# Recurrence levels of a gated linear recurrence: matmuls over the later half of each block, one copy a level, a third level buffer, and the key decays ahead of the query decays

## The chip, the cores and the metric

The kernel runs on one core of one Trainium2 chip. The metric is the device time of one execution in microseconds, the median of a few runs. The two hybrid layers of one inference step are computed in that one launch, for a prompt of 512 tokens (with 16 learned tokens ahead of it, 528 in all) and for 8 sample tokens (536 columns in all).

## The reference, cut to what matters

Each layer has a sparse attention branch and a gated linear recurrence branch (4 heads, key size 128, value size 128). The change lies in the recurrence, where a score between a query position t and an earlier key position s has its own decay for each of the 128 key dimensions:

```python
def gla_chunk(S0, q, k, v, logf):
    b = jnp.cumsum(logf.astype(jnp.float32), axis=1)
    causal = jnp.tril(jnp.ones((C, C), dtype=bool))
    diff = b[:, :, None] - b[:, None, :]
    decay = jnp.exp(jnp.where(causal[None, :, :, None, None], diff, -jnp.inf))
    scores = jnp.einsum('bthk,bshk,btshk->bths', q, k, decay)
    o = jnp.einsum('bths,bshv->bthv', scores, v) + jnp.einsum('bthk,bhkv->bthv', q * jnp.exp(b), S0)
    b_last = b[:, -1]
    S = jnp.exp(b_last)[..., None] * S0 + jnp.einsum('bshk,bshv->bhkv', k * jnp.exp(b_last[:, None] - b), v)
    return o, S
```

## The kernel before, in words

Five instruction streams (PE, DVE, ACT, POOL, SP) run a hand-written order with semaphores. A layer is: input projections (weights are split into a high and a low part, so each product is three matmuls, L695), index scores and top-k, attention, then the recurrence, the two branch projections, the output projection and the feed-forward part. The recurrence needs the whole of PE's, DVE's and ACT's attention; no projection is laid beside its level stage.

The recurrence works on chunks of 128 positions (four, and a tail of 16). `B[:, 0:4]` holds the queries, `B[:, 4:8]` the running sums of the log decays, `B[:, 8:12]` the values, `K` the keys, all with the key dimension on the partitions. The decayed scores inside a chunk are built in **levels**: `HALVES` = 64, 32, 16, 8, 4, 2, 1 are half-block sizes for levels 0 to 6, and level 7 is the diagonal, without a decay. For each level:

- DVE takes the differences of the log decays to the middle of each block: `xv[later half] = b - mid` (L2022), `xv[earlier half] = mid - b` (L2023), into the buffer `X[lev % 2]` (`X0` or `X1`);
- ACT takes the exponential of the whole buffer (L1387);
- DVE multiplies the later halves by the queries (L2034) and the earlier halves by the keys (L2035);
- PE multiplies, for each of 4 heads and 4 chunks, the 128 columns of the buffer by the same 128 columns (L1014): 16 matmuls of 128x128 by 128 columns in f32, as two groups of 8 (`hp` 0 and 1), each of which fills one PSUM work buffer of 1024 columns; a small matmul group for the tail of 16 follows at levels 3 to 7 (L1020);
- DVE copies what counts of each work buffer into `Asc` under the 8-bit mask of the level (`level_scores`, L2001, 1024 columns a copy), and the tail into `Atail` (L2008).

In the profile an f32 matmul of L1014 has two records, so a level shows as 32.

There are two work buffers of PSUM. `items` lists all their uses in order; an item takes buffer number (place % 2), and PE begins an item (`begin`) only when the item two places before it has been drained. Between the levels PE turns the values of one chunk (`v_turn`, transposes through L658), which ACT drains into `v_tok`.

DVE's order in the loop over the levels (L2011 and on) is: differences of the level, copy of the first half of the level before, then, after ACT's exponential, the two products, and the copy of the second half of the level before. At level 0 the places of the copies are taken by the low parts of the attention output (L2029) and by the diagonal.

After the last level ACT takes the exponential of the running sums into `X1` (L1401), DVE multiplies the queries by it (L2040, `q_decayed`), ACT writes 20 exponentials for the keys into the same `X1` (L1405, `k_exp`), and DVE multiplies them by the keys (L2044, `k_decayed`). PE then turns the decayed keys of chunk 0 (L658), computes the outputs of the chunk (`rec_out`, L1067 and L1068) and its state update (L1073), and one head of the sample tokens (`rank1` L1043, `rec_sample` L1051). SP loads the sample states `s0` (L501) when `k_decayed` is there, since they lie over `K`, and stores them (L388).

Each projection's gates went to DRAM; SP brings both halves back into `normed` with two DMAs (L473) early in the attention. They are first used at L2079 (half 0) and L2113 (half 1), after the recurrence.

Of the kernel before, what the change touches and what calls it, by code (L numbers as in the profile page):

```python
# [76 lines left out]
def build(nc, t, out):  # L77
# [83 lines left out]
    with ctx:  # L161
# [8 lines left out]
        normed = sb("normed", [P, 2, KT, T], f32r)  # L170
# [48 lines left out]
        base = (nc.sbuf_base + 63) // 64 * 64  # L219
        size = nc.sbuf_usable_end - base  # L220

# [50 lines left out]
        X = [X0, X1]  # L272
# [125 lines left out]
        def _(sync):  # L398
# [34 lines left out]
            with sync.Fori(0, DEPTH) as L:  # L433
# [33 lines left out]
                for n in range(4):  # L467
                    load_merge(n)
                for e in range(2):
# [20 lines left out]
                for h in range(4):  # L490
# [5 lines left out]
                    else:  # L496
# [156 lines left out]
        def _(pe):  # L653
# [16 lines left out]
            with pe.Fori(0, DEPTH) as L:  # L670
# [332 lines left out]
                for place_no, lev in enumerate(LEVELS):  # L1003
                    if lev < 7:
                        wait(pe, "lev_ready", L, 14, 2 * lev + 2)
                        left = right = X[lev % 2]
# [3 lines left out]
                    for hp in range(2):  # L1010
                        ps = begin(("level", lev, hp))
                        for m in range(8):
                            h, c = 2 * hp + m // 4, m % 4
                            mm = pe.matmul(ps[:, m * P:(m + 1) * P], left[:, h, c * P:(c + 1) * P],  # L1014
                                           right[:, h, c * P:(c + 1) * P], start=True, stop=True)
                        finish(mm, ("level", lev, hp))
# [7 lines left out]
                    if place_no < 5:  # L1024
                        r0, n = TILES[place_no]
                        ps = begin(("v_turn", place_no))
                        for h in range(4):
                            mm = transpose(ps[0:n, h * P:(h + 1) * P], B[:, 8 + h, r0:r0 + n])
                        finish(mm, ("v_turn", place_no))
                    elif place_no < 7:  # L1030
                        name, src = (("v_sample", B[:, 8:12, TP:T]), ("k_sample", K[:, :, TP:T]))[place_no - 5]
                        ps = begin(name)
                        for h in range(4):
                            mm = transpose(ps[0:NB, h * P:(h + 1) * P], src[:, h, :])
                        finish(mm, name)
# [114 lines left out]
        def _(act):  # L1150
# [26 lines left out]
            with act.Fori(0, DEPTH) as L:  # L1177
# [197 lines left out]
                for n in range(4):  # L1375
# [7 lines left out]
                    act.activation(att_hl[:, 0, n, :], A[:, n, :], ACT.Copy).then_inc(S["att_hi"], 1)  # L1383
                for lev, hs in enumerate(HALVES):
# [3 lines left out]
                    if lev < 5:  # L1388
                        n = TILES[lev][1]
                        drain_to(v_tok[0:n, lev, :], ("v_turn", lev), src=work[slot_of(("v_turn", lev))][0:n, 0:512])  # L1390
                    elif lev == 5:
                        drain_to(v_s[:, :], "v_sample", src=work[slot_of("v_sample")][0:NB, 0:512])
                    else:
# [3 lines left out]
                wait_filled(act, L, ("level_tail", 5))  # L1397
# [3 lines left out]
                act.activation(X1[:, :, :], B[:, 4:8, 0:TP], ACT.Exp).then_inc(S["decay_last"], 1)  # L1401
# [807 lines left out]
```

## Time and profile before

| | us |
|---|---|
| median of 3 runs | 2376.68 |
| lowest and highest | 2375.5, 2708.09 |
| the profiled execution, its own time | 2378.47 |
| its span, first to last instruction | 2376.5 |
| mean granted TensorE clock | 0.928 of full |

The level stage of layer 0 lies at 560.7 to 635.5 us of the span, that of layer 1 at 1721.0 to 1796.2 us. Durations are those of the one profiled execution. A row of a timeline that ends in "xN" merges N instructions: its first number is the start of the first, its second the time in which they were busy, and what is in brackets is the idle time of the engine ahead of it. "PE" are matmuls, "PEld" their weight loads, which can run under the matmuls ahead.

### The profile page before, as it was taken

What the parts mean: (1) busy time and instruction counts of PE and PEld (TensorE: products, weight loads), DVE (VectorE), ACT (ScalarE), POOL (GpSimd) and SP (SyncE); (2) the same over time, 40 slices, a digit from 0 to 9 for tenths busy, and PEclk for the clock granted to TensorE, in tenths of its full rate; (3) what the DMA queues carried; (4) which work ended last, traced back from release to release, by engine and by line L of the source; (5) the groups of instructions that cost most, each with busy time, mean ns of one, the idle gap of its engine ahead of it and who ended that gap; (6) DMA issues with size and microseconds to landing.
All of it is one profiled execution on the core that took longest, in us unless ns stands there. A gap on an engine that the chain in (4) does not pass through costs nothing.

```text
span 2376.5 us, 43282 instructions
## 1 busy us (share of the span) xinstructions
PE 2138.7 (90%) x15670; PEld 1995.6 (84%) x15670; DVE 1263.9 (53%) x2379; ACT 775.1 (33%) x1187; POOL 762.1 (32%) x414
## 2 busy tenths in 40 slices
PE   3999899886698999999999898997758989999998
PEld 2987799755588999999999778995557989999998
DVE  3475577658645643045337566875684654421433
ACT  3233222254323433222333232224522334322224
POOL 1632247200014443444355222650000344434433
PEclk9998999777879999999999799998787999999999
DMA  4322135300023322232241212432002223223322
GB/s 121 101 81 54 45 98 176 105 33 1 28 78 95 89 88 75 85 97 78 72 144 56 72 45 72 147 115 105 1 1 74 88 82 89 86 66 104 88 62 80
DMA packets 308948, 188.87 MB, mean 79 GB/s; under 512 B 15680, under 2 KB 295328, under 8 KB 307776
## 3 DMA queue, kind: packets, MB, share of 16 engines
q1 hardware_dynamic: 299168, 160.03, 23.6%
q0 software_dynamic: 4224, 16.78, 2.0%
q10 hardware_dynamic: 5408, 10.16, 1.3%
q8 instruction: 84, 1.38, 0.2%
q14 instruction: 64, 0.52, 0.1%
HBM read 167.47 MB, written 18.10 MB: 78 GB/s over the span
## 4 chain that ended last, share of the span: by engine, by line
PE 64%; issue 17%; DVE 9%; POOL 5%; ACT 3%; SPq 1%; DVEq 1%; DMA 1%; POOLq 0%; ACTq 0%
PE acc L695 49%; POOL w_lo L555 4%; PE work L658 3%; PE work L982 3%; PE work L1014 1%; PE acc L959 1%; PE work L924 1%; DVE Asc L2001 1%; POOL k_sel L621 1%; DVE std L1606 1%; ACT E L1355 1%; PE work L721 1%; PE work L1051 1%; DVE merged L2106 1%; PE work L1067 1%
## 5 line engine op out<-in xcount | busy, mean ns | idle before, releaser
L555 POOL TENSOR_TENSOR w_lo<-raw,w_hi 128x1024 fp32r<-128x1024 f32 (+3 forms) x290 | 631.1, 2177 | 1515.6 <-ACT w_hi L1193 1514.6
L695 PE MATMUL acc<-normed,w_hi 128*128 128x268 f32 x5696 | 967.1, 292 | 26.4 <-POOL w_lo L555 22.8
L695 PEld LDWEIGHTS acc<-normed,w_hi 128*128 128x128 f32 x5696 | 810.6, 192 | 58.2 <-issue 43.9
L1193 ACT ACTIVATE w_hi<-raw 128x1024 fp32r<-128x1024 f32 (+1 forms) x290 | 293.1, 1011 | 966.8 <-PE acc L695 959.4
L695 PE MATMUL acc<-normed,w_lo 128*128 128x268 f32 x2848 | 589.8, 289 | 0.0
L695 PEld LDWEIGHTS acc<-normed,w_lo 128*128 128x128 f32 x2848 | 450.9, 191 | 0.0
L695 PE MATMUL acc<-hidden,w_hi 128*128 128x268 f32 x1408 | 236.0, 290 | 16.1 <-DVE hidden L2152 16.1
L695 PEld LDWEIGHTS acc<-hidden,w_hi 128*128 128x128 f32 x1408 | 201.2, 192 | 16.9 <-issue 16.9
L695 PE MATMUL acc<-hidden,w_lo 128*128 128x268 f32 x704 | 146.4, 290 | 0.0
L2152 DVE TENSOR_TENSOR hidden<-act_f,hidden 128x536 f32 x44 | 89.5, 2033 | 54.0 <-ACT hidden L1466 54.0
L2145 DVE TENSOR_TENSOR silu<-silu,rnorm 128x536 f32<-128x536 f32 x44 | 83.4, 1896 | 59.1 <-ACT silu L1463 59.1
L695 PEld LDWEIGHTS acc<-hidden,w_lo 128*128 128x128 f32 x704 | 111.9, 192 | 0.0
L695 PE MATMUL acc<-merged,w_hi 128*128 128x268 f32 x512 | 87.1, 293 | 14.0 <-DVE merged L2106 14.0
L2127 DVE TENSOR_TENSOR x<-acc,x 128x536 f32<-128x536 f32 x32 | 22.9, 717 | 131.1 <-PE acc L695 131.1
L695 PEld LDWEIGHTS acc<-merged,w_hi 128*128 128x128 f32 x512 | 74.3, 195 | 14.4 <-issue 14.4
L2162 DVE TENSOR_TENSOR x<-acc,x 128x536 f32 x16 | 11.5, 716 | 137.6 <-PE acc L695 137.6
L1014 PE MATMUL work<-X 128*128 128x128 f32 x448 | 67.0, 321 | 17.5 <-DVE Asc L2001 17.5
L1014 PEld LDWEIGHTS work<-X 128*128 128x128 f32 x448 | 65.7, 237 | 19.1 <-DVE Asc L2001 11.3
L658 PEld LDWEIGHTS work<-cst,E 128*128 128x128 f32 (+2 forms) x240 | 26.0, 153 | 61.4 <-issue 60.9
L2142 DVE TENSOR_TENSOR silu<-acc,rnorm 128x536 f32<-128x536 f32 x44 | 31.5, 717 | 84.9 <-PE acc L695 84.1
L2148 DVE TENSOR_TENSOR act_f<-acc,silu 128x536 f32<-128x536 f32 x44 | 31.5, 716 | 80.3 <-PE acc L695 80.0
L1183 ACT ACTIVATE relu<-work 128x256 f32<-128x256 f32 (+3 forms) x64 | 33.1, 517 | 124.6 <-PE work L839 124.6
(320 smaller groups left out, 3031.9 us busy)
## 6 DMA issues: line engine op xcount, KB each, us to landing
raw<-in_w_in_dram SPq DMA_DIRECT2D x90, 512.0 KB
raw<-in_w_gu_dram SPq DMA_DIRECT2D x88, 512.0 KB
raw<-in_w_down_dram SPq DMA_DIRECT2D x32, 384.0 KB
raw<-in_w_down_dram SPq DMA_DIRECT2D x32, 320.0 KB
gate_scratch<-gate_out ACTq DMA_DIRECT2D x32, 268.0 KB
normed<-gate_scratch SPq DMA_DIRECT2D x4, 2144.0 KB, 10.7
raw<-in_w_o_dram SPq DMA_DIRECT2D x16, 512.0 KB
raw<-in_w_pa_dram SPq DMA_DIRECT2D x16, 256.0 KB
```

Source lines behind the costliest of these rows:

```text
L555: pool.tensor_tensor(w_lo[s][:, 0:kt, :], raw[slot][:, 0:kt, :], w_hi[s][:, 0:kt, :].bitcast(f32), ALU.subtract).then_inc(lo_done, 1)
L621: pool.indirect_dma_start(dst[:, i, :], None, rows, bass.IndirectOffsetOnAxis(row_idx[:, i:i + 1].bitcast(u32), 0))\
L658: return pe.transpose(dst, src, ident[0:k, 0:k])
L695: mm = pe.matmul(acc[o][:, half, 0:HT], w[s][:, k, :], mov[:, part, k0 + k, half * HT:(half + 1) * HT], start=start and n == 0, stop=stop ...
L982: mm = pe.matmul(ps[64 * s:64 * s + 64, 0:n], tok[0:w, c, 256 + n2 * 64:320 + n2 * 64], pT[0:w, s, c, 0:n], start=c == 0, stop=c == j)
L1014: mm = pe.matmul(ps[:, m * P:(m + 1) * P], left[:, h, c * P:(c + 1) * P], right[:, h, c * P:(c + 1) * P], start=True, stop=True)
L1183: act.activation(dst, ps if src is None else src, func, **kw).then_inc(drained[slot_of(item)], 1)
L1193: act.activation(w_hi[slot % 2][:, 0:kt, :], raw[slot][:, 0:kt, :], ACT.Copy).then_inc(hi_done, 1)
L2142: TT(halves(silu[:, :]), acc[0][:, :, 0:HT], halves(rnorm[:, :]), ALU.mult).then_inc(taken[0], 1)
L2145: TT(silu[:, :], silu[:, :], rnorm[:, :], ALU.mult).then_inc(S["up_scaled"], 1)
L2148: TT(halves(act_f[:, :]), acc[1][:, :, 0:HT], halves(silu[:, :]), ALU.mult).then_inc(taken[1], 1)
L2152: TT(hidden[:, 1, ds(g, 1), :].rearrange("p a t -> p (a t)"), act_f[:, :], hidden[:, 0, ds(g, 1), :].rearrange("p a t -> p (a t)").bitcast ...
```

## The change

PE's matmuls at levels 0 to 6 move only the columns of the later halves (64 of 128 for each head and chunk, taken with a stride), so a level fills one work buffer instead of two. DVE copies them with one `copy_predicated` of 1024 columns a level instead of two; its mask and its destination are taken with the same stride. The level buffers rotate over three (`X2` lies in the second half of `normed`), the differences of the next level are taken ahead of the products of this one, and the copy of a level comes after the products of the next. The gates' second half comes back only after `q_decayed`, since `X2` lies where it goes. Three `v_turn` come behind the diagonal, the other turns behind levels 0 to 3. After the levels ACT makes the key decays first, and DVE multiplies the keys before the last copy and the queries after it; the query decays go through `X2`.

```diff
-    turns = [("v_turn", c) for c in range(5)] + ["v_sample", "k_sample"]
+    TURNS = {0: [("v_turn", 0), ("v_turn", 1), ("v_turn", 2)], 1: [("v_turn", 3)], 2: [("v_turn", 4)], 3: ["v_sample"],
+             4: ["k_sample"]}
     for n, lev in enumerate(LEVELS):
-        items += [("level", lev, 0), ("level", lev, 1)] + ([("level_tail", lev)] if lev >= 3 else []) + turns[n:n + 1]
+        items += [("level", 7, 0), ("level", 7, 1)] if lev == 7 else [("level", lev)]
+        items += ([("level_tail", lev)] if lev >= 3 else []) + TURNS.get(n, [])
...
+        X2 = nc.alloc_sbuf_tensor_at("X2", [P, 4, TP], f32, offset=base_n + KT * TB)
+        X = [X0, X1, X2]
...
-                for e in range(2):
-                    sync.dma_start(normed[:, e, :, :].bitcast(f32), gate_dram[:, :, e, :].rearrange("g p t -> p g t"))\
-                        .then_inc(S[f"gate_back{e}"], 16)
+                gate_return(0)
...
+                    if h == 1:
+                        wait(sync, "q_decayed", L, 1, 1)
+                        hold(sync)
+                        gate_return(1)
                     if h >= 1:
                         store_state(sync, L, h - 1)
...
+                        left = right = X[lev % 3]
+                        ps, hs = begin(("level", lev)), HALVES[lev]
+                        for m in range(16):
+                            h, c = m // 4, m % 4
+                            late = right[:, h, c * P:(c + 1) * P].rearrange("p (b t) -> p b t", t=2 * hs)[:, :, hs:]
+                            mm = pe.matmul(ps[:, m * 64:(m + 1) * 64].rearrange("p (b t) -> p b t", t=hs),
+                                           left[:, h, c * P:(c + 1) * P], late, start=True, stop=True)
+                        finish(mm, ("level", lev))
...
                 for lev, hs in enumerate(HALVES):
                     w = 512 if hs >= 16 else TP
                     wait(act, "lev_diff", L, 14, 2 * lev + 2)
-                    act.activation(X[lev % 2][:, :, 0:w], X[lev % 2][:, :, 0:w], ACT.Exp).then_inc(S["lev_exp"], 1)
+                    act.activation(X[lev % 3][:, :, 0:w], X[lev % 3][:, :, 0:w], ACT.Exp).then_inc(S["lev_exp"], 1)
+                    if lev == 0:
+                        for c in range(3):
+                            v_drain(c)
...
-                wait_filled(act, L, ("level_tail", 5))
+                wait_filled(act, L, ("level_tail", 4))
...
-                act.activation(X1[:, :, :], B[:, 4:8, 0:TP], ACT.Exp).then_inc(S["decay_last"], 1)
-                wait(act, "q_decayed", L, 1, 1)
                 for c, (r0, n) in enumerate(TILES):
                     for h in range(4):
                         act.activation(X1[:, h, r0:r0 + n], B[:, 4 + h, r0:r0 + n], ACT.Exp, scale=-1.0,
                                        bias=B[:, 4 + h, r0 + n - 1:r0 + n]).then_inc(S["k_exp"], 1)
+                wait_filled(act, L, ("level_tail", 5))
+                act.activation(X2[:, :, :], B[:, 4:8, 0:TP], ACT.Exp).then_inc(S["decay_last"], 1)
...
+                def level_scores(lev):
+
+                    hs = HALVES[lev]
+                    ps = wait_filled(vec, L, ("level", lev))
+                    hold(vec)
+                    late = level_mask[:, lev, :].rearrange("p (b t) -> p b t", t=2 * hs)[:, :, hs:]
+                    drain_ins(vec.copy_predicated(
+                        Asc[:, :, :].rearrange("p h (c b t) -> p (h c) b t", c=4, t=2 * hs)[:, :, :, hs:],
+                        late.unsqueeze(1).broadcast_to((P, 16, 64 // hs, hs)),
+                        ps[:, :].rearrange("p (m b t) -> p m b t", m=16, t=hs)), ("level", lev))
+                    if lev >= 3:
+                        tail_scores(lev)
...
+                level_diff(0)
+                for n in range(4):
+                    wait(vec, "att_hi", L, 4, n + 1)
+                    TT(att_hl[:, 1, n, :], A[:, n, :], att_hl[:, 0, n, :].bitcast(f32), ALU.subtract)\
+                        .then_inc(S["att_lo"], 1)
+                wait(vec, "att_lo", L, 4, 4)
+                hold(vec)
+                level_diff(1)
+                wait(vec, "scores_cleared", L, 2, 2)
+                diagonal(0)
+                diagonal(1)
+                tail_scores(7)
+                level_product(0)
+                for lev in range(1, 7):
+                    if lev < 6:
+                        level_diff(lev + 1)
+                    level_product(lev)
+                    level_scores(lev - 1)
                 wait(vec, "lev_ready", L, 14, 14)
-                wait(vec, "decay_last", L, 1, 1)
-                TT(B[:, 0:4, 0:TP], X1[:, :, :], B[:, 0:4, 0:TP], ALU.mult).then_inc(S["q_decayed"], 1)
-                level_scores(6, 0)
-                level_scores(6, 1)
                 wait(vec, "k_exp", L, 20, 20)
                 TT(X1[:, :, :], X1[:, :, :], K[:, :, 0:TP], ALU.mult).then_inc(S["k_decayed"], 1)
+                level_scores(6)
+                wait(vec, "decay_last", L, 1, 1)
+                TT(B[:, 0:4, 0:TP], X2[:, :, :], B[:, 0:4, 0:TP], ALU.mult).then_inc(S["q_decayed"], 1)
```

`level_diff` and `level_product` hold the same two instructions each as before (L2022, L2023 and L2034, L2035), and `diagonal` the copy of level 7.

## Rows read from the trace of the kernel before

**Rows 1.** The page's busy shares, and one of its costliest groups (parts 1 and 5).

```profile
PE 2138.7 (90%) x15670; PEld 1995.6 (84%) x15670; DVE 1263.9 (53%) x2379; ACT 775.1 (33%) x1187; POOL 762.1 (32%) x414
...
L2001 DVE COPY_PREDICATED Asc<-level_mask,work 128x1024 f32<-128x1024 uint8 x32 | 41.2, 1295 | 12.1 <-PE work L1014 12.1
```

**Rows 2.** Windows of both stages: length, busy PE, PEld, DVE, ACT, POOL, clock, DMA, GB/s.

```profile
560.70:635.50 74.80, 40.67 (x301) 38.37 (x300) 60.63 (x56) 25.38 (x37) 0.00 (x0) 0.80 0.00 1
1721.00:1796.20 75.20, 39.38 (x296) 37.29 (x297) 60.84 (x57) 25.38 (x37) 0.00 (x0) 0.82 0.00 1
```

**Rows 3.** Timeline around the matmuls of level 1, layer 0.

```profile
579.54 3.84 PE L1014 MATMUL work<-X 128*128 128x128 f32 x32 [2.72 <-DVE Asc L2001]
...
581.74 1.33 DVE L2001 COPY_PREDICATED Asc<-level_mask,work 128x1024 f32<-128x1024 uint8 x1
581.76 1.91 ACT L1387 ACTIVATE X<-X 128x2048 f32<-128x2048 f32 x1 [4.31 <-DVE X L2023]
...
583.71 1.23 DVE L2034 TENSOR_TENSOR X<-X,proj_rec 128x1024 f32<-128x1024 f32 x1 [0.64 <-ACT X L1387]
...
585.99 1.28 DVE L2001 COPY_PREDICATED Asc<-level_mask,work 128x1024 f32<-128x1024 uint8 x1
```

**Rows 4.** Windows of L924's matmuls (4 moved columns) alone: length, busy, clock, DMA.

```profile
433.70:437.50 3.80, 3.80 (x36) 1.00 0.19 74
438.00:443.20 5.20, 5.20 (x26) 0.50 0.17 50
```

**Rows 5.** Timeline of L1051 (1 moved column), clock 1.00 and 0.50.

```profile
649.17 1.95 PE L1051 MATMUL work<-proj_rec,s 128*128 128x1 f32 x16
...
678.18 3.57 PE L1051 MATMUL work<-proj_rec,s 128*128 128x1 f32 x16
```

**Rows 6.** Windows of L1014's matmuls alone, with the same columns.

```profile
571.00:574.20 3.20, 3.01 (x15) 0.50 0.00 0
579.60:583.10 3.50, 3.50 (x31) 1.00 0.00 0
588.10:591.20 3.10, 3.10 (x17) 0.50 0.02 5
612.70:617.50 4.80, 4.60 (x32) 0.74 0.02 3
```

**Rows 7.** Timeline of the stage's start.

```profile
560.73 1.22 DVE L2022 TENSOR_TENSOR X<-proj_rec 128x1024 f32<-128x1024 f32 x1
...
563.00 2.59 DVE L2029 TENSOR_TENSOR att_hl<-proj_att,att_hl 128x536 fp32r<-128x536 f32 x4
...
570.29 1.11 PE L658 MATMUL work<-cst,proj_rec 128*128 128x128 f32 x4 [3.05 <-DVE Asc L2001]
...
571.44 0.60 ACT L1183 ACTIVATE v_tok<-work 128x512 f32<-128x512 f32 x1 [6.41 <-PE work L658]
```

**Rows 8.** Timeline of the stage's end.

```profile
621.39 5.37 PE L1014 MATMUL work<-X 128*128 128x128 f32 x32
...
626.75 5.57 ACT L1405 ACTIVATE X<-proj_rec 128x128 f32<-128x128 f32 x20 [2.50 <-DVE proj_rec L2040]
...
632.35 2.36 DVE L2044 TENSOR_TENSOR X<-X,K 128x2112 f32<-128x2112 f32 x1 [3.15 <-ACT X L1405]
...
635.53 0.55 PEld L1067 LDWEIGHTS work<-Asc,v_tok 128*128 128x128 f32 x2
```

**Rows 9.** Three lines: duration min/median/max in ns, first and last start, forms.

```profile
L1014 PE MATMUL work<-X x448: 273/275/426, 571.2 to 1787.1; 128*128 128x128 f32 x150
...
L1051 PE MATMUL work<-proj_rec,s x128: 250/250/373, 649.2 to 1842.0; 128*128 128x1 f32 x128
...
L2022 DVE TENSOR_TENSOR X<-proj_rec x14: 1205/1240/1247, 560.7 to 1773.5; 128x1056 f32<-128x1056 f32 x8, 128x1024 f32<-128x1024 f32 x6
```

**Rows 10.** DMA issues: size of each, median time from issue to landing.

```profile
normed<-gate_scratch SPq DMA_DIRECT2D x4, 2144.0 KB, 10.7
...
out_dram<-s SPq DMA_DIRECT2D x8, 512.0 KB, 4.0
```

More of the change, by code:

```diff
@@ L468, in _, with gate_return @@
                     load_merge(n)
+                def gate_return(e):
+                    sync.dma_start(normed[:, e, :, :].bitcast(f32), gate_dram[:, :, e, :].rearrange("g p t -> p g t"))\
+                        .then_inc(S[f"gate_back{e}"], 16)
                 for e in range(2):
@@ L1005, in _ @@
                         wait(pe, "lev_ready", L, 14, 2 * lev + 2)
-                        left = right = X[lev % 2]
+                        hold(pe)
+                        left = right = X[lev % 3]
[6 more added lines that the diff above has]
+                        finish(mm, ("level", lev))
                     else:
@@ L1009, in _ @@
                         left, right = K, B
[L1010 to L1016, printed above, removed]
+                        for hp in range(2):
+                            ps = begin(("level", lev, hp))
+                            for m in range(8):
+                                h, c = 2 * hp + m // 4, m % 4
+                                mm = pe.matmul(ps[:, m * P:(m + 1) * P], left[:, h, c * P:(c + 1) * P],
+                                               right[:, h, c * P:(c + 1) * P], start=True, stop=True)
+                            finish(mm, ("level", lev, hp))
                     if lev >= 3:
@@ L1022, in _ @@
                         finish(mm, ("level_tail", lev))
[L1024 to L1031, printed above, removed]
-                        ps = begin(name)
-                        for h in range(4):
-                            mm = transpose(ps[0:NB, h * P:(h + 1) * P], src[:, h, :])
+                    for name in TURNS.get(place_no, ()):
+                        ps = begin(name)
+                        if name[0] == "v_turn":
+                            r0, n = TILES[name[1]]
+                            for h in range(4):
+                                mm = transpose(ps[0:n, h * P:(h + 1) * P], B[:, 8 + h, r0:r0 + n])
+                        else:
+                            src = B[:, 8:12, TP:T] if name == "v_sample" else K[:, :, TP:T]
+                            for h in range(4):
+                                mm = transpose(ps[0:NB, h * P:(h + 1) * P], src[:, h, :])
                         finish(mm, name)
@@ L1995, in _, with diagonal @@
                 vo.settle()
-                def level_scores(lev, hp):
-                    ps = wait_filled(vec, L, ("level", lev, hp))
+                def diagonal(hp):
+                    ps = wait_filled(vec, L, ("level", 7, hp))
                     hold(vec)
@@ L2012, in _ @@
[L2012 to L2020 removed]
+                        level_mask[:, 7:8, :].broadcast_to((P, 8, P)),
@@ L2021, in _, with level_views, level_diff @@
+                def level_views(lev):
+                    hs, w = HALVES[lev], (512 if HALVES[lev] >= 16 else TP)
+                    return [src[:, :, 0:w].rearrange("p h (b c) -> p h b c", c=2 * hs)
+                            for src in (X[lev % 3], B[:, 4:8, :], B[:, 0:4, :], K)] + [hs, w]
+                def level_diff(lev):
+                    xv, bv, qv, kv, hs, w = level_views(lev)
                     mid = bv[:, :, :, hs - 1:hs].broadcast_to((P, 4, w // (2 * hs), hs))
@@ L2023, in _, with level_product @@
                     TT(xv[:, :, :, 0:hs], mid, bv[:, :, :, 0:hs], ALU.subtract).then_inc(S["lev_diff"], 1)
-                    if lev >= 1:
-                        level_scores(lev - 1, 0)
-                    else:
-                        for n in range(4):
-                            wait(vec, "att_hi", L, 4, n + 1)
-                            TT(att_hl[:, 1, n, :], A[:, n, :], att_hl[:, 0, n, :].bitcast(f32), ALU.subtract)\
-                                .then_inc(S["att_lo"], 1)
-                        wait(vec, "scores_cleared", L, 2, 2)
-                        level_scores(7, 0)
+                def level_product(lev):
+                    xv, bv, qv, kv, hs, w = level_views(lev)
                     wait(vec, "lev_exp", L, 7, lev + 1)
```

42 lines of the change are left out of this document (17 added, 25 removed).

## Prediction

> **What bounds the kernel now.** The page's shares come first: PE is at work for 90% of the span, DVE for 53% [rows 1]. That average is made by the projections; the change touches only the level stage, so I went to the windows of it: 74.8 and 75.2 us of the span [rows 2], 150 in all, with DVE busy for 60.6 us of each, PE for 40, ACT for 25, POOL for none. Nothing else runs beside it, so what the stage loses the kernel loses one for one, and what it gains comes back whole: PE's next work waits for its end.
>
> Inside, the timeline shows a chain that goes round between DVE and PE [rows 3]: PE waited 2.72 us for a copy before its level, DVE 0.64 for ACT's exponential. Level 1's matmuls start at 579.54 [rows 3], level 6's at 621.39 [rows 8], so five periods take 41.85 us, 8.4 each. DVE's own work in one is four differences or products (1.22 each, some 1.13 to 1.17 from start to start, since the end of one lies under the next) and two copies (1.28, some 1.18 so): 6.9 us.
>
> **What a matmul costs here.** This decides the case. A level has 32 records. At clock 1.00 they take 3.84 us with the last one's 0.275: (3.84 - 0.275)/31 = 0.115 us a record [rows 3, 9]. L1051 moves one column, not 128, against weights of the same 128x128: (1.95 - 0.25)/15 = 0.113 at clock 1.00, (3.57 - 0.37)/15 = 0.213 at 0.50 [rows 5, 9]. L924 moves 4: 36 records in 3.80 us at 1.00, 26 in 5.20 at 0.50, where one or two are counted over at the edges [rows 4]. With 128 columns at 0.50 it is 17 in 3.10 us, without the two at the edges 0.21 [rows 6]. So the record costs 0.113 or 0.213 us by clock alone, whatever it moves: the weight load sets it, and the change leaves all 32 loads. Halving the moved columns I cost at nothing; bounds: 0 and, if the time went by half the columns, 1.8 us a level at full clock, 3.4 at half. The rows at 1 and 4 columns enclose 64 with the row at 128, so I take 0.
>
> The Trainium skill (TensorE: Matmul & The Clock Gate, "Back-to-back issue gap") gives an isolated matmul a gap of N/2.4 + 2.5 ns, so going from 128 to 64 columns would save 27 ns a record, by my estimate 12 us over both layers; the 0.113 at one column speaks against using it here, where each matmul has a weight load of its own.
>
> **The clock.** It is here that the columns matter. L924's stream kept PE full of weight loads with hardly a column moved: its clock was 1.00 at 433.7 to 437.5 and 0.50 at 438.0 to 443.2, without a pause between [rows 4]. Streams of L1014 with 128 columns did the reverse: after 0.50 at 571.0 to 574.2 the next level ran at 1.00, and within one level of 4.80 us the mean was 0.74, low first and high behind [rows 6]. So loads do not raise the clock and columns do. 64 columns lie between, no row shows them. At 0.50 a level of 128 columns streams without a pause; one of 64 will move for about half of each 0.213. I take it that this does not bring the clock back, which is nearer to L924 than to a full stream, and that it stays at 0.50 for most of the stage.
>
> **The change part by part, at layer 0's times.**
> Start: differences of level 0 at 560.73, the four low parts until 565.51 [rows 7], differences of level 1 (2 x 1.13) until 567.9, two diagonal copies and the tail until 570.4, products of level 0 until 572.7. PE's three turns take 4 x 0.213 each from 570.4, ACT's drains 0.60 each [rows 7], and level 0 follows the drain of the second at 573.05 (before, right behind one turn, at 571.2 [rows 9]).
> Three turns in a row are 2.6 us of unbroken 128-column moves right ahead of it, not much less than the 3.2 us at 0.50 in rows 6; I expect them to bring the clock up once, about 1.3 us into level 0 (an estimate). Then: rest of level 0 at 0.113, DVE's copy not before its products of level 1, which wait for the second exponential until 575.7, so the copy is at 578.0 to 579.2; level 1 starts at 579.25, half of it at high clock: 16 x 0.113 + 16 x 0.213 + 0.4 = 5.6, its copy ends at 586.2.
> From there PE bounds. With one work buffer a level, and levels 0 to 3 all in the same one (two items apart), PE can't begin a level while the last is copied: 7.2 us (32 x 0.213 + 0.39, between the two lines' longest) + copy 1.28 + 0.08 of hand-over = 8.56 a level. This is the serial chain that the two half groups avoided. DVE has 5.8 us of work in it (four at 1.17 and one copy), so the exponential (1.91) and the removed 1.18 of copying, 8.3 us a layer, lie in its idle time. Level 2 begins at 586.3, level 3 at 594.8, level 4 at 604.0 (8.56, and 0.6 for the k_sample turn, which goes ahead of it), level 5 at 612.6, level 6 at 621.1, and its matmuls end at 628.3.
> End: ACT's 5.57 us of key exponentials start behind the tail of level 4 and are hidden, and so are the keys' product and X2's exponential. What is left: copy 1.28, tail 0.12, queries' product 2.36 and 0.1: 632.2 against 635.53 before, where after the last level's matmuls (626.8) came 5.57 + 2.36 and the turn [rows 8]. Saved: 3.4 us a layer, 6.8 in both.
> Strided access: DVE's differences run at inner runs of 64 down to 1 column and take 1.205 to 1.247 us over all 14 [rows 9], so a stride costs f32 nothing. For the mask of bytes no row shows it; bounds: 0 (the f32 row, nearest, which I take) and a doubling, +1.2 a copy. A strided moved operand could cost twice and still lie under the load.
> SP: the key product is earlier, so the s0 loads are. Then SP waits for `q_decayed`, with the first s0 store, the loads of the other two heads and the weight loads queued behind it. The gate return takes 10.7 us and a store 4.0 [rows 10], 14.7 even one after the other. The load of the third head waits in any case for L1051's first run, which ended at 651.1 [rows 5], 15.6 us after the outputs began at 635.53 [rows 8]. Cost 0; if DMAs run late, up to 2 us a layer. Half 1 of the gates is used only behind all chunks and the first branch projection. Early in the attention one DMA less runs; nothing on the path waited for it.
>
> **Sum.** The profiled execution took 2378.5; minus 6.8 is 2371.7. It was 1.8 above the median of the runs, so 2370 for the median.
>
> **The rivals.**
> A, the clock stays high. Then DVE bounds at 5.8 us a level, PE's 3.9 lie under it, the last two levels go by PE (3.9 + 1.36), and the output starts at about 615.3: 20 us a layer, 2337. For it: gaps of 1.4 us between bursts, where now PE idles 2.72 and the level behind still runs at 1.00 [rows 3, 6]. Against it: L924, with no gap at all. The Trainium skill (same page, "Why this matters for your kernels") says the clock holds when PE isn't left idle for long between bursts; by that rule 2337 is the result. L924 disagrees.
> B, slower: the serial chain of PE and copy decides, with the clock low throughout and byte masks at a stride costing double. It starts to decide as soon as the period passes the old mean of about 8.4: low clock alone gives 8.56 and +0.6 us a layer (2378), each 0.1 us on a copy adds 1.4 in both layers, the doubling 17: 2395. For it: one buffer a level; against: the f32 strides.
> C, halved columns halve the record after all. The period falls to DVE's 5.8 at either clock, which ends where A does; [rows 4, 5] speak against it.
>
> **How the numbers follow.** Forecast 0.66 (its own range 2362 to 2380, from one more or one less stretch at high clock), A 0.15, C 0.03, B 0.12, something else 0.04. The range must take in half of A and reach over the low end of B: 2336 to 2386. Two per cent, about what a measurement of this kernel can tell from no change, is 48 us: faster needs more than A, slower more than B: 0.04 and 0.02, within 0.94.
>
> **What would show it.** L1014 (64 columns) at 32 records a level with 0.113 or 0.213 each; granted clock near 0.5 in most of the stage; DVE's copy waiting for PE at levels 1 to 6, about 2.5 us each; DVE's busy time about 8 us less a stage; no waits at ACT's exponential; key exponentials ahead of the last levels' end. Wrong would be: records below 0.09, a clock of 1.00 across several levels, copies above 1.4 us, or SP's store landing late.

## The result and the profile after

The changed kernel takes 2387.87 us (median of 18 runs, 2374.11 to 2394.96), the kernel before 2376.24 (18 runs) on the same chip: ratio 1.0044, 95% interval 1.0031 to 1.0056. It is slower by a small but measured amount, where a gain of 6 us was forecast. The profiled execution took 2389.42 us with a span of 2387.6.

First the page of the changed kernel, which answers to [rows 1] and [rows 10]:

```profile
PE 2176.8 (91%) x15670; PEld 2030.3 (85%) x15670; DVE 1249.6 (52%) x2365; ACT 774.1 (32%) x1187; POOL 762.2 (32%) x414
...
L1024 PE MATMUL work<-X 128*128 128x64 f32 x448 | 94.5, 406 | 11.5 <-DVE Asc L2046 11.5
...
normed<-gate_scratch SPq DMA_DIRECT2D x4, 2144.0 KB, 8.4
```

PE has as many instructions as before and is busy for 38 us more, though 448 of its matmuls move half the columns. DVE is busy for 14 us less, as intended, and the kernel gains nothing from it. The gate return lands as fast as it did.

Next its windows of the level stage and of the chunk loop behind it (from the first output's weight load or matmul to the first branch projection), both layers; columns as in [rows 2]:

```profile
564.90:638.80 73.90, 53.60 (x296) 50.01 (x296) 53.58 (x49) 25.44 (x38) 0.00 (x0) 0.57 0.05 15
638.80:689.40 50.60, 48.61 (x217) 41.39 (x217) 18.78 (x56) 5.53 (x12) 0.00 (x0) 0.63 0.36 112
1723.90:1801.60 77.70, 58.30 (x296) 54.55 (x296) 53.64 (x49) 25.43 (x38) 0.00 (x0) 0.51 0.05 14
1801.60:1850.70 49.10, 46.52 (x217) 39.19 (x217) 18.80 (x56) 5.52 (x12) 0.00 (x0) 0.67 0.37 115
```

The stage was 74.8 and 75.2 us at a clock of 0.80 and 0.82 [rows 2]; now DVE has 7 us less to do in it (53.6 for 60.6), PE 13 to 19 us more, and the clock is 0.57 and 0.51. The chunk loops, in which the change touches only one DMA (the second gate return), took 46.1 and 46.0 us at a clock of 0.72 before; they have 4.5 and 3.1 us more. Taken together, (73.9 + 77.7 + 50.6 + 49.1) - (74.8 + 75.2 + 46.1 + 46.0) = 9.2 us, of the 11.1 between the two spans (2387.6 - 2376.5).

The timeline of layer 0's levels, PE and DVE around levels 0, 3, 5 and 6, answers to [rows 3] and [rows 8]:

```profile
577.40 4.34 PE L1024 MATMUL work<-X 128*128 128x64 f32 x32
...
599.22 7.09 PE L1024 MATMUL work<-X 128*128 128x64 f32 x32 [0.60 <-DVE Asc L2046]
...
615.63 1.23 DVE L2046 COPY_PREDICATED Asc<-level_mask,work 128x1024 f32<-128x1024 uint8 x1 [1.93 <-PE work L1024]
616.08 5.57 ACT L1429 ACTIVATE X<-proj_rec 128x128 f32<-128x128 f32 x20
616.92 7.09 PE L1024 MATMUL work<-X 128*128 128x64 f32 x32 [1.11 <-DVE Asc L2046]
624.16 2.44 DVE L2046 COPY_PREDICATED Asc<-level_mask,work 128x1024 f32<-128x1024 uint8 x1 [4.84 <-PE work L1024]
626.65 7.09 PE L1024 MATMUL work<-X 128*128 128x64 f32 x32 [2.32 <-DVE Asc L2046]
633.90 2.42 DVE L2046 COPY_PREDICATED Asc<-level_mask,work 128x1024 f32<-128x1024 uint8 x1 [5.05 <-PE work L1024]
636.25 2.32 DVE L2096 TENSOR_TENSOR proj_rec<-X,proj_rec 128x2112 f32<-128x2112 f32 x1
638.81 0.79 PE L1086 MATMUL work<-Asc,v_tok 128*128 128x128 f32 x2 [1.32 <-DVE proj_rec L2096]
```

A level of 32 records is 7.09 us: (7.09 - 0.39)/31 = 0.216 us a record, the low clock's price. Levels 1, 2, 3, 5 and 6 each wait for the copy of the level before, since they need the same buffer, and each copy waits for the matmuls: the serial chain. ACT's key exponentials lie under level 5, as meant. And at levels 5 and 6 the copy takes twice as long as at level 4. The group of the copy shows that it is these alone (duration min/median/max in ns; first and last start):

```profile
L2046 DVE COPY_PREDICATED Asc<-level_mask,work x14: 1226/1286/2442, 582.4 to 1796.7; 128x1024 f32<-128x1024 uint8 x14
```

### The profile page after: what moved, and what is told of

It is laid out like the page before. It is cut to its first block, busy times and chain, and to the rows that moved or that the text cites. A ratio compares the mean times of both kernels' runs of the same rounds, so it can differ in the third digit from the quotient of the medians.

```text
span 2387.6 us, 43254 instructions
## 1 busy us (share of the span) xinstructions
PE 2176.8 (91%) x15670; PEld 2030.3 (85%) x15670; DVE 1249.6 (52%) x2365; ACT 774.1 (32%) x1187; POOL 762.2 (32%) x414
## 4 chain that ended last, share of the span: by engine, by line
PE 66%; issue 17%; DVE 7%; POOL 5%; ACT 2%; SPq 1%; DVEq 1%; DMA 1%; POOLq 0%; ACTq 0%
PE acc L707 49%; POOL w_lo L567 4%; PE work L1024 4%; PE work L670 3%; PE work L994 2%; PE acc L971 1%; PE work L936 1%; POOL k_sel L633 1%; DVE std L1632 1%; PE work L1086 1%; DVE Asc L2046 1%; ACT E L1374 1%; PE work L1087 1%; PE work L733 1%; DVE merged L2158 1%
## 5 line engine op out<-in xcount | busy, mean ns | idle before, releaser
L1024 PEld LDWEIGHTS work<-X 128*128 128x128 f32 x448 | 92.5, 319 | 15.0 <-DVE Asc L2046 14.5
L1024 PE MATMUL work<-X 128*128 128x64 f32 x448 | 94.5, 406 | 11.5 <-DVE Asc L2046 11.5
```

The lines of the kernel that those rows point to most:

```text
L1024: mm = pe.matmul(ps[:, m * 64:(m + 1) * 64].rearrange("p (b t) -> p b t", t=hs), left[:, h, c * P:(c + 1) * P], late, start=True, stop=True)
```

## The experiments

Two theories were set against each other first. Theory 1: moving 64 columns instead of 128 keeps TensorE's clock at its lower level through the levels, and that is the loss; the new order of the work gains. Its rival: the serial chain of one buffer a level is the loss, and the columns are indifferent. Four kernels put order, columns and copies together differently.

**sched128**: the changed kernel's order, third buffer and decay order, with 128 columns moved and whole copies, two half groups a level as before.

```diff
-                        ps, hs = begin(("level", lev)), HALVES[lev]
-                        for m in range(16):
...
+                        for hp in range(2):
+                            ps = begin(("level", lev, hp))
+                            for m in range(8):
+                                h, c = 2 * hp + m // 4, m % 4
+                                mm = pe.matmul(ps[:, m * P:(m + 1) * P], left[:, h, c * P:(c + 1) * P],
+                                               right[:, h, c * P:(c + 1) * P], start=True, stop=True)
```

> The changed kernel's order (third buffer, differences ahead, key decays first, turns) with the matmuls of 128 columns and the two full copies of before: the order alone. Theory 1: clock mostly 1.00, DVE bounds at 7.0 us a level, 10 to 14 us a layer less than before, 2348 to 2360. If the order itself had cost time (later start, the returned gates, the turns in a row), it would be at 2376 or above.

**late128**: as sched128, but each half's copy takes the later halves only (512 columns) at levels 0 to 4.

```diff
+                        if hs > 2:
+                            late = level_mask[:, lev, :].rearrange("p (b t) -> p b t", t=2 * hs)[:, :, hs:]
+                            drain_ins(vec.copy_predicated(
+                                Asc[:, 2 * hp:2 * hp + 2, :].rearrange("p h (c b t) -> p (h c) b t", c=4, t=2 * hs)[:, :, :, hs:],
+                                late.unsqueeze(1).broadcast_to((P, 8, 64 // hs, hs)),
+                                ps[:, :].rearrange("p (m b t) -> p m b t", m=8, t=2 * hs)[:, :, :, hs:]), ("level", lev, hp))
```

> The changed kernel, but PE moves all 128 columns of each level buffer into the two half groups of before, and DVE copies only the later halves of each group (512 columns twice; at levels 5 and 6 the full 1024 twice). Theory 1 (the moved columns decide the clock, the weight load decides the record): the granted clock is 1.00 over most of the level stage, records cost 0.113 us, DVE bounds at about 6 us a level, the stage is 57 us instead of 74 to 78, and the time 2340 to 2355. Rival (one work buffer a level makes PE and copy a serial chain, and the clock is a side effect of the pauses): about the same 2340 to 2360 here, so this run alone doesn't tell them apart; late64 beside it does.

**late64**: as late128, with 64 columns moved into the first 512 columns of each buffer; the groups, their order and the two buffers stay.

```diff
-                                mm = pe.matmul(ps[:, m * P:(m + 1) * P], left[:, h, c * P:(c + 1) * P],
-                                               right[:, h, c * P:(c + 1) * P], start=True, stop=True)
+                                late = right[:, h, c * P:(c + 1) * P].rearrange("p (b t) -> p b t", t=2 * hs)[:, :, hs:]
+                                mm = pe.matmul(ps[:, m * 64:(m + 1) * 64].rearrange("p (b t) -> p b t", t=hs),
+                                               left[:, h, c * P:(c + 1) * P], late, start=True, stop=True)
```

> Same as late128 in groups, buffers and order, but PE moves only the 64 later columns in each of the 8 matmuls of a group, and every copy takes 512 columns. Theory 1: the clock falls to 0.50 for nearly the whole stage, a level costs PE 6.8 us, period 7.7 to 8.2, time 2370 to 2390, 25 to 40 us above late128. Rival (serial chain): two groups in two buffers as in late128, so within 5 us of late128.

**cols_only**: the kernel before, with its own order, and of the change only the 64 moved columns and the one copy a level.

```diff
+                        for m in range(16):
+                            h, c = m // 4, m % 4
+                            late = right[:, h, c * P:(c + 1) * P].rearrange("p (b t) -> p b t", t=2 * hs)[:, :, hs:]
+                            mm = pe.matmul(ps[:, m * 64:(m + 1) * 64].rearrange("p (b t) -> p b t", t=hs),
+                                           left[:, h, c * P:(c + 1) * P], late, start=True, stop=True)
```

> The kernel before with the 64-column matmuls and the single copy alone (two level buffers, old order, old turns, old decays). Theory 1: clock 0.50 in most of the stage, and the copy, the products and PE's 7.2 us follow one another: 10 to 11 us a level instead of 8.4, time 2400 to 2415. Rival (the columns are a gain or nothing, the loss comes from the new order): 2365 to 2378.

Measured, with the kernel before at 2376.74 us in the same runs; the changed kernel's row is from its own (stages and chunk loops of the profiled execution, layer 0 and 1):

| kernel | order | columns | us | ratio, 95% interval | stages | chunk loops |
|---|---|---|---|---|---|---|
| before | old | 128 | 2376.7 | 1 | 74.8, 75.2 | 46.1, 46.0 |
| cols_only | old | 64 | 2410.1 | 1.0127 (1.0094 to 1.016) | 90.2, 90.3 | 48.1, 48.2 |
| sched128 | new | 128 | 2353.1 | 0.9892 (0.9868 to 0.9915) | 65.0, 64.9 | 46.0, 46.1 |
| late128 | new | 128 | 2347.0 | 0.9861 (0.9835 to 0.9887) | 57.5, 57.4 | 49.9, 49.0 |
| late64 | new | 64 | 2371.2 | 0.9982 (0.9965 to 0.9998) | 72.7, 69.3 | 46.0, 48.7 |
| changed | new | 64 | 2387.9 | 1.0044 (1.0031 to 1.0056) | 73.9, 77.7 | 50.6, 49.1 |

late128 and late64 differ in the moved columns, and in how the copies of levels 5 and 6 are laid, which take 1.29 us a half in both. The same level (level 3, layer 0) in their timelines, late128 first:

```profile
597.88 3.84 PE L1024 MATMUL work<-X 128*128 128x128 f32 x32
```

```profile
597.55 7.09 PE L1026 MATMUL work<-X 128*128 128x64 f32 x32
```

Twice the columns take 3.84 us at the full clock, half of them 7.09 us at the lower one: (3.84 - 0.275)/31 = 0.115 against 0.216 us a record, the two prices that [rows 3 to 5] had. The narrow version is 24 us slower. The rival falls: late64 has no one-buffer chain (no copy holds up its matmuls at levels 0 to 3) and still runs at the lower clock. On the old order, too, 64 columns with one copy a level are a loss (33 us; cols_only brings the one buffer and the doubled copies along, so not all of it is the clock's): its levels took 7.06 us each and DVE stood idle for 69 us behind PE in both layers.

That the price goes by the clock and not by the columns is seen where narrow matmuls met the full clock. Level 0 of layer 1 in dest_flat (a variant below), at a granted clock of 0.98:

```profile
1729.43 3.84 PE L1024 MATMUL work<-X 128*128 128x64 f32 x32
```

The same 3.84 us as with 128 columns. But no narrow kernel kept that clock. In 16 stages of the eight profiles with 64 columns it was up at levels 0 or 1 in six (layer 0 of the changed kernel, layer 1 of late64, both of alternate and of dest_flat), and back at 0.50 within level 2 at the latest in all six.

The order alone (sched128) gains 24 us, of which the forecast had seen only its 6.8, net of the low clock. In late128 the windows show what bounds the stage once the clock is high:

```profile
566.70:624.20 57.50, 36.38 (x296) 33.06 (x296) 54.28 (x56) 25.33 (x38) 0.00 (x0) 0.88 0.06 18
```

DVE is busy for 54.3 of 57.5 us, PE for 36.4 only, so here time off DVE can count, as long as nothing else gets longer by it. The copies of 512 columns show the first such saving (first group: levels 0 to 4; second: whole copies at 5 and 6):

```profile
L2048 DVE COPY_PREDICATED Asc<-level_mask,work x20: 679/693/725, 584.1 to 1748.7; 128x512 f32<-128x512 uint8 x20
...
L2053 DVE COPY_PREDICATED Asc<-level_mask,work x8: 1282/1292/1297, 613.4 to 1758.7; 128x1024 f32<-128x1024 uint8 x8
```

5 levels x 2 halves x 0.6 = 6 us a layer off the bounding engine; the stage is 7.5 us shorter than sched128's. The chunk loops gave half of these 15 us back (49.9 and 49.0 for 46.0 and 46.1); the medians lie 6 us apart.

**alternate**: is the one-buffer chain worth anything beside the clock? The turns are moved so that levels 0 to 5 lie in the two buffers by turns.

```diff
-    TURNS = {0: [("v_turn", 0), ("v_turn", 1), ("v_turn", 2)], 1: [("v_turn", 3)], 2: [("v_turn", 4)], 3: ["v_sample"],
-             4: ["k_sample"]}
+    TURNS = {0: [("v_turn", c) for c in range(5)], 4: ["v_sample"], 5: ["k_sample"]}
```

(Keys of TURNS are places in the order of the levels; place 0 is the diagonal.)

> Changed kernel with the seven turns placed so that successive levels use different work buffers (five value turns behind the diagonal, the two sample turns behind levels 3 and 4 in the order of the levels), all else the same, 64 columns moved. A level's matmuls then need not wait for the copy of the level before. Theory 1 (the low clock of narrow matmuls sets the level at 7.1 us, and one buffer adds 1.3 to 1.5 us a level): period about 7.2 to 7.9 us instead of 8.6 where clock is 0.50, stage shorter by 3 to 6 us a layer, 2376 to 2382 us. Rival (the one-buffer chain was the whole loss, and closing it lets the clock rise): levels at clock 1.00, 3.8 us each, 2350 to 2360 us.

Measured 2377.05 us, ratio 0.9997 (0.9981 to 1.0013), stages of 72.2 and 72.2 us: by the ratios 0.0047 or 11 us less than the changed kernel. Levels 2 and 3 now stream without a pause, at the lower clock:

```profile
584.67 13.89 PE L1023 MATMUL work<-X 128*128 128x64 f32 x64 [0.93 <-DVE X L2071]
```

64 records in 13.89 us, so closing the chain did not bring the clock back; the rival's 2350 to 2360 falls. The time hit the forecast of the first theory, but mostly by another way than the one it named: against a stage of the changed kernel without a stretch at the high clock (77.7 us) this one is 5.5 us shorter, and 5.1 of them are the clock's, since levels 0 and 1 took 4.28 and 4.72 us for 7.04 and 7.09 (within 0.02 us the same in layer 1). Closing the chain saved 1.7 us where it shows undisturbed (level 3 began 6.85 us behind level 2, for 8.54), but two more turns ahead of level 0 made it begin 1.75 us later, which took most of the chain's part back.

**mask_packed, dest_flat**: what doubles the copies of levels 5 and 6? First the mask's later halves are packed side by side, then, instead, the destination of these two levels is laid without gaps.

```diff
-            vec.tensor_copy(level_mask[:, :, :], level_f[:, :, :])
+            for lev, hs in enumerate(HALVES):
+                vec.tensor_copy(level_mask[:, lev, 0:64].rearrange("p (b t) -> p b t", t=hs),
+                                level_f[:, lev, :].rearrange("p (b t) -> p b t", t=2 * hs)[:, :, hs:])
```

```diff
+                    if hs <= 2:
+                        dst = Asc[:, 0:2, :].rearrange("p h (m b t) -> p (h m) b t", m=8, t=hs)
```

> Changed kernel with one thing altered: the later halves of each level's byte mask lie side by side in their row, so the level copies read the mask without gaps; Asc, the destination, keeps its gaps of 2 and of 1 column at levels 5 and 6. Theory 2a (the mask's short runs of bytes double the copy): the copies of levels 5 and 6 fall from 2.44 to about 1.25 us, 4 copies x 1.2 = 4.8 us less, ratio about 1.0024, 2383 us beside a before of 2377. Theory 2b (the short runs of the float destination double it): copies still 2.4 us, ratio about 1.0044, 2387 us. Matmuls stay 7.1 us a level at clock 0.50 in both.

> Changed kernel with the destination of the copies of levels 5 and 6 laid into the first 1024 columns of Asc without gaps (the scores of these two levels then stand in wrong columns; nothing is left out); the mask keeps its gaps, and the work buffer is read without gaps as before. The packed mask left these copies at 2.44 us. If the gaps of the float destination double them: 1.25 us here, 4 x 1.2 us less, about 2382 us. If neither side alone does it, or the mask's gaps suffice too: 2.4 us still, about 2387.

The groups of the copy, of mask_packed and of dest_flat:

```profile
L2051 DVE COPY_PREDICATED Asc<-level_mask,work x14: 1226/1293/2439, 579.0 to 1802.1; 128x1024 f32<-128x1024 uint8 x14
```

```profile
L2050 DVE COPY_PREDICATED Asc<-level_mask,work x14: 1227/1287/1300, 576.9 to 1785.7; 128x1024 f32<-128x1024 uint8 x14
```

Packing the mask changes no copy, and laying the destination flat takes all of them to 1.30 us or less, with the mask's gaps still there. So the gaps of the float destination double the copy, at runs of 2 and of 1 column and not at 4 or more, and the mask's gaps are indifferent. mask_packed's time, 2381.13 us (ratio 1.0022, 1.0009 to 1.0036), looks like the other theory's forecast, but its copies say no: a time that fits is not yet the cause. Its profiled execution took 77.8 us for each stage, no less than the changed kernel's; one chunk loop fell out at 46.0 instead of 49 us. That execution, at 2391.83 us, was the slowest of the twelve, so what brought the median down is in no profile and stays open. dest_flat took 2376.50 us in its one run (changed kernel beside it 2387.24, also one), with stages of 72.4 and 72.7 us: 4.8 us of that gain are the copies, most of the rest the clock, which came up into levels 0 and 1 in both layers.

The Trainium skill (SBUF — State Buffer, "Door 1: The DMA port swizzle") says that SBUF has lines of 16 bytes, four fp32 values, that accesses reach full bandwidth with two or more hits a line, and that each new line costs. The doubling sets in between runs of 4 and of 2 columns, where only half of each line comes to be used. But two columns of every line are used at runs of 2 and of 1 alike, which the clause on two hits lets pass, and DVE's differences, whose destination has the same gaps, stay at 1.24 us. So the rule alone doesn't tell what the copy costs; its 2.44 us decides.

**tail128**: levels 5 and 6 of the changed kernel moved at 128 columns in two half groups and copied whole, levels 0 to 4 left narrow. It asks what decides the chunk loop behind the levels.

```diff
-        items += [("level", 7, 0), ("level", 7, 1)] if lev == 7 else [("level", lev)]
+        items += [("level", lev, 0), ("level", lev, 1)] if lev in (5, 6, 7) else [("level", lev)]
```

> Changed kernel, but levels 5 and 6 move all 128 columns in four groups of eight and are copied whole (1.29 us a half, as in the 2353.14 us version); levels 0 to 4 keep 64 columns. What is open: the chunk loop behind the levels took 50.6 and 49.1 us in the changed kernel's profile (clock 0.63 and 0.67) against 46.1 and 46.0 before (0.72), yet 49.9 and 49.0 also in the 2346.96 us version, whose levels run at the full clock. Theory A (the clock at the end of the levels decides the chunk loop): both chunk loops 46.0 us here, and with levels 5 and 6 at 3.8 to 5.5 us and the doubled copies gone, 5 to 8 us less a layer: 2370 to 2377. Theory B (the chunk loop's clock falls out one way or the other in each execution, with the kernel or without): 46 to 50.6 us mixed, and 3 to 6 us less a layer from the two levels alone: 2374 to 2382.

Measured 2374.89 us, ratio 0.9993 (0.9977 to 1.0008): 12 us less than the changed kernel. Level 4, 5 and 6 of layer 0:

```profile
607.69 6.92 PE L1034 MATMUL work<-X 128*128 128x64 f32 x32
...
616.06 5.81 PE L1026 MATMUL work<-X 128*128 128x128 f32 x32 [1.12 <-DVE Asc L2067]
...
623.38 3.84 PE L1026 MATMUL work<-X 128*128 128x128 f32 x32 [1.22 <-DVE Asc L2058]
```

Within one level of 128-column matmuls the clock came up, and the next ran at it throughout, with the same pauses ahead (1.12 and 1.22 us). That is the columns' effect within one execution. But the chunk loops behind took 48.5 and 49.6 us, not 46.0: Theory A falls, and B fits. (The time, 2374.89 us, lies in both forecasts; the loops tell them apart.)

**pool_diff**: late128 with the early halves' subtraction given to GpSimd, to take DVE down.

```diff
+                    wait(pool, "lev_diff", L, 7, lev + 1)
+                    hold(pool)
+                    pool.tensor_tensor(xv[:, :, :, 0:hs], mid, bv[:, :, :, 0:hs], ALU.subtract).then_inc(S["lev_pool"], 1)
```

> The 2346.96 us version, with the early halves' subtraction of each level (1056 or 1024 columns, 1.25 us on DVE) given to GpSimd, which has no work in that stage. If DVE, busy 54 of the stage's 57.5 us, is what bounds it once the clock is high: 6 levels x 1.2 = 7 us less a layer, less what GpSimd's longer subtraction (2.4 us for 1024 columns in its rows of this trace) delays the first level: 5 to 7 us a layer, 2333 to 2338. Rival (GpSimd beside DVE slows DVE's operations, or the clock falls because TensorE's groups stand otherwise): operations on DVE over 1.35 us instead of 1.25, or levels at 7 us; 2345 to 2360.

**late128_packed**: late128 with the packed mask and 512-column copies at levels 5 and 6 too.

> The version of 2346.96 us (later halves copied, 128 columns moved, four groups of eight records in two buffers), with the packed mask and 512-column copies at levels 5 and 6 too, read from psum at a stride. Theory 2a: these copies take 0.70 us instead of 1.29, 8 fewer halves x 0.6 = 4.7 us less on a DVE that is busy 54 of the 57.5 us of the stage: 2342 us. Theory 2b: they take 1.30 us as before and nothing changes, 2347 us.

pool_diff: 2343.51 us, ratio 0.9868 (0.9842 to 0.9894), the same as late128's 0.9861. Its windows, DVE and GpSimd (third and fifth busy columns), and the group of the product that follows the exponential:

```profile
561.30:620.20 58.90, 38.09 (x296) 34.65 (x296) 49.30 (x49) 26.72 (x39) 13.77 (x7) 0.85 0.06 18
```

```profile
L2089 DVE TENSOR_TENSOR X<-X,proj_rec x14: 1206/1344/1841, 570.5 to 1746.1; 128x1056 f32<-128x1056 f32 x8, 128x1024 f32<-128x1024 f32 x6
```

DVE is busy for 5 us less and the stage is 1.4 us longer: the chain over GpSimd (1.95 us a subtraction) and the exponential (1.95) now comes last, with DVE idle for 8.8 us behind L1424's exponentials in layer 0, and a product beside GpSimd takes up to 1.84 us instead of 1.25. So the gain went to the rival's first half, slower operations on DVE beside GpSimd, and to the longer chain, which the forecast had counted for the first level only; its second half, the clock, took no part (0.85 for 0.88). late128_packed: 2341.68 us, ratio 0.986 (0.9839 to 0.9881), stages of 57.3 us, copies of levels 5 and 6 at 1.29 us for 512 columns. Theory 2b, as dest_flat has it: half the columns at double price. Its 5 us against late128's median are not in the ratio, and its chunk loops were 46.1 and 47.0 us in the profile, for 49.9 and 49.0. Here too the time is what the other theory forecast (2342), and the copies say no.

**after_again, before_again**: both kernels once more, unchanged, for a second profile.

> The changed kernel once more, for its profile. In the first one layer 0's stage took 73.9 and layer 1's 77.7 us, and the chunk loops 50.6 and 49.1. If these differences between like stages belong to the kernel they come again within 0.5 us. If the clock falls out differently in each execution (what the other runs' chunk loops of 46.0 to 50.5 us suggest), the stages and the chunk loops come out otherwise: stages between 73 and 78, chunk loops between 46 and 51 us, the levels behind level 0 at 7.1 us and clock 0.50 in both.

> The kernel before once more, for its profile: stages of 74.8 and 75.1 us and chunk loops of 46.1 and 46.0 in the first. If its clock falls in one way each time: the same within 0.5 us. If it falls out in each execution as in the others: chunk loops of 46 to 50, with a time between 2371 and 2385.

The changed kernel's two stages, then the kernel before's two stages and two chunk loops:

```profile
557.80:635.50 77.70, 58.29 (x296) 54.55 (x296) 53.63 (x49) 25.43 (x38) 0.00 (x0) 0.51 0.05 14
1721.70:1799.40 77.70, 58.30 (x296) 54.55 (x297) 53.63 (x49) 25.43 (x38) 0.00 (x0) 0.51 0.05 14
```

```profile
567.10:641.90 74.80, 40.27 (x296) 38.16 (x297) 60.65 (x56) 25.38 (x37) 0.00 (x0) 0.80 0.00 1
1727.40:1802.50 75.10, 39.50 (x296) 37.42 (x297) 60.77 (x56) 25.38 (x37) 0.00 (x0) 0.80 0.00 1
641.90:688.00 46.10, 43.97 (x218) 37.07 (x217) 18.15 (x56) 6.12 (x13) 0.00 (x0) 0.72 0.34 98
1802.50:1848.60 46.10, 43.98 (x219) 37.08 (x217) 18.17 (x56) 6.12 (x13) 0.00 (x0) 0.72 0.35 98
```

The kernel before repeats itself to 0.1 us in both places; its 2384.83 us instead of 2378.5 had come up elsewhere, most of it ahead of the attention, whose first matmul stood at 467.6 instead of 461.4 us. The changed kernel doesn't: layer 0's stage was 73.9 us with one stretch at the high clock in levels 0 and 1, and is 77.7 us without it (level 0 of 7.03 instead of 4.34 us); its chunk loops were 49.0 and 49.1 us, at 0.67. Stages and chunk loops together are 253.5 us against the 242.1 of the kernel before: 11.4 us, the difference of the medians being 11.6. The two single executions lay only 2.4 us apart, for what the kernel before had lost elsewhere.

## Why the prediction was wrong

What held, by its steps:

- **The record.** 0.113 or 0.213 us by clock alone, halved columns nothing: 0.115 us at the full clock with 128 columns and with 64, 0.216 at the lower. Rival C falls.
- **The clock.** "64 columns don't bring it back": all levels behind level 1 at 0.50 in four stages of four. Rival A falls for this kernel. Its 2337 was, for the version that keeps 128 columns, about right (2347).
- **The serial chain.** Levels 2 and 3 began 8.54 us apart (590.68 and 599.22); 8.56 forecast. Counted from the stage's start, levels 1 to 5 began within 0.4 us of the forecast.
- **The covers.** Key exponentials, gate return and store cost nothing; DVE was idle for PE behind each level. (sched128 has the same gate return, and its chunk loops took 46.0 and 46.1 us as before.)

What failed, against the sum of 2371.7 for the profiled execution, which was 2389.4, 17.7 more:

- **The strided copies, 0 in the sum.** The argument was that DVE's f32 differences run through the same gaps at 1.24 us, with the byte mask as the unknown. The price was real at two levels of seven (2.44 and 2.42 for 1.25 us) and lay in the float destination. "Copies above 1.4 us" stood among its own signs of being wrong. Both stand on the serial chain: 1.2 x 2 levels x 2 layers = 4.8 us. With them layer 0's stage is forecast at 71.4 + 2.4 = 73.8; it was 73.9.
- **The one stretch at the high clock, taken for both layers.** It came in one stage of the four. Without it the stage is 73.9 + 3.8 = 77.7 us: 3.8 us in layer 1, 7.6 in the second profile.
- **The chunk loop, not in the sum at all.** The working ended at the first output's matmul. But the loop's length, too, goes by the clock: 46.0 us at 0.72, 50.6 at 0.63. It took 7.6 us more (4.5 and 3.1) in the first profile and 5.9 in the second (98.1 against 92.2). A change that moves the clock has to be followed until it is back.

These are 4.8 + 3.8 + 7.6 = 16.2 of the 17.7 us; the rest lies outside stages and loops, where the kernel before alone wanders by 6 us from one execution to the next. Rival B had the right sign and the first two mechanisms, but its doubling was priced for all copies, and it had 0.12 where the forecast had 0.66. The range failed by the same omission: its upper end took nothing in for what follows the stage.

The larger error of reading shows only in sched128: the order alone gained 24 us. The forecast's low clock was right, but it was the change's own price, 24 us by the pair late128 and late64, not a state that the stage had anyway.

What stays open is why the chunk loop falls out at 46.0, 47 to 49 or 50 us. The clock in the levels doesn't decide it alone: late128, at the full clock in most levels, had 49.9 and 49.0, and late64, at the lower, 46.0 in one layer. In all four loops of the kernel before and both of sched128 it was 46.0 to 46.1, in all four of the changed kernel 49.0 to 50.6. So is why the clock came up at level 0 in one narrow stage and not in the next of the same kernel: no run asks it.

The Trainium skill (TensorE: Matmul & The Clock Gate, "Why this matters for your kernels") ties the loss of the clock to pauses between bursts. Each stage does start with a long one (10.01 us ahead of the diagonal's tail in the changed kernel, 9.99 in late128). Behind it, narrow matmuls lost the clock again or never had it, with pauses of 0.6 to 2.3 us or with none (the 13.89 us stream), while late128 had it in most levels with pauses of up to 1.8 us. That rule would have given 2337 us; of the pair, the one that moved more had the clock.

## What to carry to other kernels

Where the weight load sets a matmul's time, moving fewer columns saves nothing and can cost TensorE its clock: change what DVE copies and leave what PE moves; that version (late128, ratio 0.9861; 0.986 with the packed mask) beats both kernels. Forecast such a change by a pair of whole stretches at either clock, and follow the clock past the end of the stage. And read a copy's cost at its shortest inner run, by its destination, before it is put on a serial chain.

## What was unexpected of the hardware

- COPY_PREDICATED with an f32 destination in SBUF takes 1.23 to 1.30 us for 1024 columns with inner runs of 4 or more, and 2.42 to 2.44 with runs of 2 or 1 (0.68 to 0.73 and 1.30 for 512). TENSOR_TENSOR with the same gaps in sources and destination takes 1.21 to 1.25 us at every run. The byte mask's gaps cost nothing.
- 32 f32 matmuls with a weight load each take 3.84 us with 128 moved columns and 7.09 with 64 in otherwise equal kernels. At one clock they cost the same (3.84 us with 64 at 0.98); the narrow ones did not keep it.
- A DVE product of 1056 columns that overlapped a GpSimd subtraction of as many took up to 1.84 us instead of 1.25.
